# The per-layer projection placed ahead of the gate product

## The reference, cut to what matters

```python
h = h + 0.5 * rmsnorm_2(swiglu(rmsnorm_2(h, norm_g[0]), ffn1_gu, ffn1_down), norm_g[1])
...                                     # the token mixer, norms 2 and 3
h = h + 0.5 * rmsnorm_2(swiglu(rmsnorm_2(h, norm_g[4]), ffn2_gu, ffn2_down), norm_g[5])
gate = jax.nn.sigmoid(rmsnorm_2(h, norm_g[6]) @ ple_gate)
h = h + rmsnorm_2((p_i @ ple_proj) * gate, norm_g[7])
```

## Time and profile before

| | |
|---|---|
| median of 3 runs | 2860.72 us (2858.97 to 2862.37) |
| the profiled execution | 2861.04 us |
| its span in the trace | 2858.9 us |
| mean granted TensorE clock | 0.966 of full |
| TensorE busy | 2662.3 us, 12320 products |
| POOL, DVE, ACT busy | 1037.0, 1144.5, 979.3 us |

### The profile page before, as it was taken

How to read it: one execution, slowest core, us unless ns; L and a number is a source line. 1 busy time by engine, 2 the same in 40 slices (tenths; PEclk the granted TensorE clock), 3 DMA queues, 4 the chain that set the end, 5 groups by cost and what they waited for, 6 DMA issues and landing times.

```text
span 2858.9 us, 32128 instructions
## 1 busy us (share of the span) xinstructions
PE 2662.3 (93%) x12320; PEld 2111.7 (74%) x12320; DVE 1144.5 (40%) x1735; ACT 979.3 (34%) x1419; POOL 1037.0 (36%) x444
## 2 busy tenths in 40 slices
PE   8899988888999999879999998999998969999996
PEld 2788766676888877657888876788877747888875
DVE  0788665524222036555222035322027574322025
ACT  2323323423323233444233234323233444323233
POOL 0223255433444432213444433444432203444432
PEclk9999999999999999979999999999999979999998
DMA  6212110032332322102333322333322102332321
GB/s 262 60 59 90 51 37 30 24 106 74 103 103 89 96 81 72 52 23 75 102 96 96 93 91 68 103 96 96 96 89 65 60 8 81 96 99 93 102 90 66
DMA packets 63331, 234.00 MB, mean 82 GB/s; under 512 B 7264, under 2 KB 7520, under 8 KB 62688
## 3 DMA queue, kind: packets, MB, share of 16 engines
q1 hardware_dynamic: 61056, 222.33, 24.6%
q10 hardware_dynamic: 2144, 9.80, 1.0%
HBM read 230.00 MB, written 2.10 MB: 81 GB/s over the span
## 4 chain that ended last, share of the span: by engine, by line
issue 58%; POOL 20%; PE 16%; DVE 3%; ACT 1%; DMA 1%; POOLq 1%; SPq 0%; DVEq 0%; ACTq 0%
POOL wlo L448 20%; PE banks L1904 2%; PE banks L1910 2%; PE banks L1905 2%; PE banks L1842 1%; PE banks L2024 1%; DMA ada_raw<-in_stream 1%; PE banks L1680 1%; PE banks L2031 1%; PE banks L1973 1%; PE banks L1975 1%; PE banks L1974 1%; PE banks L1908 1%; PE banks L1909 1%; PE banks L1994 1%
## 5 line engine op out<-in xcount | busy, mean ns | idle before, releaser
L448 POOL TENSOR_TENSOR wlo<-raw,whi 128x1024 fp32r<-128x1024 f32 x351 | 848.4, 2421 | 1418.7 <-ACT whi L478 1418.6
L1650 PE MATMUL banks<-xhi,whi 128*128 128x512 f32 x2016 | 800.4, 397 | 60.5 <-ACT xhi L502 30.1
L1651 PE MATMUL banks<-xhi,wlo 128*128 128x512 f32 x2016 | 793.1, 393 | 0.0
L1660 PE MATMUL banks<-xlo,whi 128*128 128x512 f32 x2016 | 762.3, 394 | 5.7 <-DVE xlo L983 5.7
L478 ACT ACTIVATE whi<-raw 128x1024 fp32r<-128x1024 f32 x396 | 415.6, 1054 | 375.6 <-PE banks L1660 367.6
L1650 PEld LDWEIGHTS banks<-xhi,whi 128*128 128x128 f32 x2016 | 383.3, 190 | 157.5 <-issue 57.0
L1660 PEld LDWEIGHTS banks<-xlo,whi 128*128 128x128 f32 x2016 | 380.2, 189 | 94.2 <-DVE xlo L983 11.9
L1651 PEld LDWEIGHTS banks<-xhi,wlo 128*128 128x128 f32 x2016 | 383.7, 190 | 80.0 <-issue 1.3
L1650 PE MATMUL banks<-act_hi,whi 128*128 128x512 f32 x704 | 273.9, 389 | 0.0
L1651 PE MATMUL banks<-act_hi,wlo 128*128 128x512 f32 x704 | 273.9, 389 | 0.0
L1660 PE MATMUL banks<-act_lo,whi 128*128 128x512 f32 x704 | 273.9, 389 | 0.0
(11 more groups left out here) (368 smaller groups left out, 3140.1 us busy)
## 6 DMA issues: line engine op xcount, KB each, us to landing
raw<-in_stream SPq DMA_DIRECT2D x396, 512.0 KB, 3.5
ada_raw<-in_stream SPq DMA_DIRECT2D x24, 512.0 KB, 9.1
h<-in_x ACTq DMA_DIRECT2D x2, 2048.0 KB, 12.2
out<-h SPq DMA_DIRECT2D x4, 512.0 KB, 2.6
ctx_raw<-in_ctx ACTq DMA_DIRECT2D x1, 1024.0 KB, 19.5
dft_t<-in_dft_t ACTq DMA_DIRECT2D x1, 1024.0 KB, 4.8
ple_raw<-in_ple ACTq DMA_DIRECT2D x2, 512.0 KB, 3.5
mixpar<-in_mixpar ACTq DMA_DIRECT2D x2, 384.0 KB, 4.1
```

What stands on the lines that cost most here:

```text
L448: pool.tensor_tensor(wlo[:, i], raw[:, i], whi[:, i].bitcast(F32), ALU.subtract)\
L1650: pe.matmul(acc[acc_of[t]][:], whi[:, u % SLOTS, i], x_h, start=(k == 0), stop=False)
L1651: pe.matmul(acc[acc_of[t]][:], wlo[:, u % SLOTS, i], x_h, start=False, stop=False)
L1660: mm = pe.matmul(acc[acc_of[t]][:], whi[:, u % SLOTS, i], x_l, start=False, stop=(k == k_tiles - 1))
```

## The change

The projection goes ahead of the gate product, behind the down product of s = 2. TensorE runs two of its tiles, then the sum of squares of the down output, then the other six tiles. DVE copies each projection tile out of PSUM into a new buffer `projected_ple` before it begins `boundary`. `ple` is loaded at the start of s = 2 into other memory, and `ple_hi` and `ple_lo` are made during the gate-up tiles of s = 2 (pairs 4 and 6). In s = 3 DVE scales each gate tile straight into `y_dyn`, ACT takes the sigmoid in place, DVE multiplies by `projected_ple` one tile behind, and ACT squares one tile behind; the table for Ln and Exp is loaded again behind the last sigmoid. In `norm_in` the gate's units are cast behind the projection's.

```diff
     STREAM += [(("gu", _layer, 0), 2 * FT, KT), (("down", _layer, 0), KT, FT),
                (("in2", _layer), IN_T, KT), (("out2", _layer), KT, KT),
                (("gu", _layer, 1), 2 * FT, KT), (("down", _layer, 1), KT, FT),
-               (("gate", _layer), KT, KT), (("proj", _layer), KT, PLE_T)]
+               (("proj", _layer), KT, PLE_T), (("gate", _layer), KT, KT)]
 WHOLE_UNITS = ADA_T * KT // UNIT
...
         mod_rows = at("mod_rows", DYN + 25 * KB, [D * 3])
         c_silu = at("c_silu", DYN + 24 * KB, [KT, 2])
-        ple_raw = at("ple_raw", DYN + 16 * KB, [PLE_T, SEQ])
-        ple_hi = at("ple_hi", DYN + 20 * KB, [PLE_T, SEQ], F32R)
-        ple_lo = at("ple_lo", DYN + 24 * KB, [PLE_T, SEQ], F32R)
+        ple_raw = at("ple_raw", 36 * KB, [PLE_T, SEQ])
+        ple_hi = at("ple_hi", 40 * KB, [PLE_T, SEQ], F32R)
+        ple_lo = at("ple_lo", 44 * KB, [PLE_T, SEQ], F32R)
+        projected_ple = at("projected_ple", DYN + 16 * KB, [KT, SEQ])
         ident = table[:, C_ID:C_ID + P]
         ones = table[:, C_ONE:C_ONE + P]
...
             def norm_in(q, gain):
+                if q[1] == 3:
+                    high_parts(units_to(q))
                 high_parts(units_to(q) + SLOTS)
                 for k in range(KT):
                     if k == 5:
...
             for layer in range(DEPTH):
                 for s in range(4):
                     q = (layer, s)
-                    if s == 3:
+                    if s == 2:
                         act.dma_start(ple_raw[:, :, :], a["ple"][layer].rearrange("p (k t) -> p k t", t=SEQ))\
                             .then_inc(ld[f"ple{layer}"], 16)
...
                             act.activation(tmp[0][:], tmp[0][:], ACT.Silu).then_inc(*done("silu", (q, j)))
                             act.wait_ge(*after("act_formed", (q, j)))
                             act.activation(act_hi[:, j], tmp[1][:], ACT.Copy).then_inc(*done("act_high", (q, j)))
+                            if s == 2 and j == 4:
+                                act.wait_ge(ld[f"ple{layer}"], 16)
+                                act.activation(ple_hi[:, :, :], ple_raw[:, :, :], ACT.Copy)\
+                                    .then_inc(*done("ple_high", layer))
                         y_out(("down", layer, s // 2), q, FT, y_over_x)
                     elif s == 1:
...
                     else:
                         for m in range(KT):
                             tile_ready(("gate", layer), m, KT)
-                            if m == 3:
-                                act.wait_ge(ld[f"ple{layer}"], 16)
-                                act.activation(ple_hi[:, :, :], ple_raw[:, :, :], ACT.Copy)\
-                                    .then_inc(*done("ple_high", layer))
                             act.wait_ge(*after("gate2_scaled", (layer, m)))
-                            act.activation(y_dyn[:, m], tmp[m % 2][:], ACT.Sigmoid)\
+                            act.activation(y_dyn[:, m], y_dyn[:, m], ACT.Sigmoid)\
                                 .then_inc(*done("gate2", (layer, m)))
+                            if m:
+                                act.wait_ge(*after("y_formed", (q, m - 1)))
+                                squares("y_sq", q, m - 1, y_dyn[:, m - 1])
                         log_and_exp()
-                        for m in range(KT):
-                            tile_ready(("proj", layer), m, PLE_T)
-                            act.wait_ge(*after("y_formed", (q, m)))
-                            squares("y_sq", q, m, y_dyn[:, m])
+                        act.wait_ge(*after("y_formed", (q, KT - 1)))
+                        squares("y_sq", q, KT - 1, y_dyn[:, KT - 1])
                         inverse_root((("post", q), D, norm_bank[:], inv_rms[:]))
             high_parts(units)
...
                         boundary("first", None, q, par1[:, P1_FIN:P1_FIN + KT], gains(layer, 2 * s))
                     else:
                         y = y_over_x if before[1] in (0, 2) else y_dyn
+                        if s == 3:
+                            for m in range(KT):
+                                t = first_tile["proj", layer] + m
+                                v.wait_ge(*after("product", (("proj", layer), m)))
+                                v.tensor_copy(projected_ple[:, m], acc[acc_of[t]][:]).then_inc(*done("ple_out", (layer, m), bank_of=t))
                         boundary(before, y, q, gains(before[0], 2 * before[1] + 1), gains(layer, 2 * s))
                     if s == 1:
                         hgrn_clear(layer)
...
                             v.wait_ge(*after("act_high", (q, j)))
                             v.tensor_tensor(act_lo[:, j], tmp[1][:], act_hi[:, j].bitcast(F32), ALU.subtract)\
                                 .then_inc(*done("act_low", (q, j)))
+                            if s == 2 and j == 6:
+                                v.wait_ge(*after("ple_high", layer))
+                                v.tensor_tensor(ple_lo[:, :, :], ple_raw[:, :, :], ple_hi[:, :, :].bitcast(F32),
+                                                ALU.subtract).then_inc(*done("ple_low", layer))
                         for m in range(KT):
                             sq_add("y_sq", q, m)
                     elif s == 1:
...
                         for m in range(KT):
                             sq_add("y_sq", q, m)
                     else:
+                        def gated(m):
+                            v.wait_ge(*after("gate2", (layer, m)))
+                            v.tensor_tensor(y_dyn[:, m], y_dyn[:, m], projected_ple[:, m], ALU.mult)\
+                                .then_inc(*done("y_formed", (q, m)))
+                            if m:
+                                sq_add("y_sq", q, m - 1)
+
                         for m in range(KT):
                             t = first_tile["gate", layer] + m
                             v.wait_ge(*after("product", (("gate", layer), m)))
-                            if m >= 2:
-                                v.wait_ge(*after("gate2", (layer, m - 2)))
-                            v.tensor_tensor(tmp[m % 2][:], acc[acc_of[t]][:], inv_rms[:], ALU.mult)\
+                            v.tensor_tensor(y_dyn[:, m], acc[acc_of[t]][:], inv_rms[:], ALU.mult)\
                                 .then_inc(*done("gate2_scaled", (layer, m), bank_of=t))
-                            if m == 4:
-                                v.wait_ge(*after("ple_high", layer))
-                                v.tensor_tensor(ple_lo[:, :, :], ple_raw[:, :, :], ple_hi[:, :, :].bitcast(F32),
-                                                ALU.subtract).then_inc(*done("ple_low", layer))
-                        for m in range(KT):
-                            t = first_tile["proj", layer] + m
-                            v.wait_ge(*after("product", (("proj", layer), m)))
-                            v.wait_ge(*after("gate2", (layer, m)))
-                            v.tensor_tensor(y_dyn[:, m], y_dyn[:, m], acc[acc_of[t]][:], ALU.mult)\
-                                .then_inc(*done("y_formed", (q, m), bank_of=t))
                             if m:
-                                sq_add("y_sq", q, m - 1)
+                                gated(m - 1)
+                        gated(KT - 1)
                         sq_add("y_sq", q, KT - 1)
                     before = q
             boundary(before, y_dyn, "last", gains(DEPTH - 1, 7), None)
...
                         product(("out2", layer), KT, KT, xhi, xlo, "mix", lambda k: (layer, k))
                     else:
                         product(("gate", layer), KT, KT, xhi, xlo, "x", tile, pre_sum, True)
-                        product(("proj", layer), KT, PLE_T, ple_hi, ple_lo, "ple", lambda k: layer)
-                    sum_squares(("post", q), "y_sq", q)
+                    if s == 2:
+                        post_sum = lambda m: sum_squares(("post", q), "y_sq", q) if m == 1 else None
+                        product(("proj", layer), KT, PLE_T, ple_hi, ple_lo, "ple", lambda k: layer, after_tile=post_sum)
+                    else:
+                        sum_squares(("post", q), "y_sq", q)
     return ev.values, ev.freed
...
             if s == 0:
                 weights.append(leads_first(blocks_of(i["w_in_2"][l][:, order])))
                 weights.append(blocks_of(i["w_out_2"][l][order_out]))
+        weights.append(blocks_of(i["ple_proj_2"][l]))
         weights.append(leads_first(blocks_of(i["ple_gate_2"][l])))
-        weights.append(blocks_of(i["ple_proj_2"][l]))
     par = np.zeros((DEPTH, P, P2_COLS), np.float32)
     mix = np.zeros((DEPTH, P, M2_COLS), np.float32)
     for l in range(DEPTH):
```

## The result

The kernel after takes **2866.9 us** (median of 20 executions, 2865.2 to 2874.8), the one before 2861.3 us in the same sessions (20 executions, 2856.8 to 2864.7). The medians differ by 5.6 us, where 5.4 were forecast. The ratio is 1.0025 with a 95% interval of 1.0019 to 1.0032, about 7 us. It lies above the quotient of the medians because five of the 20 executions after took 2873 to 2875 us, which a median doesn't see; the means differ by 7.4 us. The execution that was profiled after the change took 2870.4 us (span 2868.6), 3.5 more than its median; the one before took 2861.04. The traces have therefore 9.4 us to account for, not 5.6.

The account below looks back on a forecast made before the run. TensorE, busy 93% of the span, was taken to bound the kernel. Per layer -0.9 - 0.05 + 1.2 + 1.7 + 0.8 = +2.7, two layers +5.4 on the 2860.72 us median: 2866.1 us, range 2857 to 2870.

Parts of the forecast that it names:

- The move: Projection put behind the down product: 10.89 us go at layer end, first residual step +9.9 later; -0.9 us a layer.
- The held first addition: Seam: DVE's addition of k=0 waits for a whole POOL subtraction; TensorE restarts 4.6 us behind the first residual step.
- First step to tile 4: First residual step to gate tile 4: 30.7 us, -0.1 us for both layers together, bounds -2.9 to +2.
- The casts moved into s = 2: `ple_hi` and `ple_lo` at gate-up pairs 4 and 6 cost nothing; without idle cover, 2.6 us a layer.
- The sixth cast: Gate stage: squares delay ACT's cast of the sixth unit, so `wlo` and tile 5 come +1.2 us late a layer.
- the clock behind tile 5: After a 2.5 us wait at gate tile 5, 3.4 us at half clock lose +1.7 us a layer.
- The tail: Last gate product to Ln: 7.0 us where last projection product to Ln was 6.14; +0.8 us a layer.
- The copies did not wait for POOL: Rival on the moved projection: PSUM copies do wait for POOL, +1.6 us a layer, 2869.3 us; chance 0.10.
- Square and sigmoid need no load between them: Rival on the gate: square and sigmoid need different tables, each alternation loads 1.3 us, 2878.5 us; chance 0.05.
- No fall at tile 5: Rival: clock does not fall behind gate tile 5's wait, all else as forecast, +2.0, 2862.7 us; chance 0.18.
- The sum: All terms: +2.7 us a layer, +5.4 for two; 2866.4 us for the profiled execution, 2866.1 for the median; chance 0.50.
- the gate's terms: Gate stage a layer: +1.2 us for the late sixth unit and +1.7 us for half clock behind tile 5.

Follow-up runs that it names:

- Experiment 2: Kernel after, with ACT's cast of the gate's third unit moved behind the input casts of k=0 and k=1: 2866.3 us, ratio 1.0012 to the kernel before.
- experiment 3: Kernel after, with ACT casting the gate's sixth unit right behind the first sigmoid: 2862.0 us, ratio 1.0001 to the kernel before.
- experiment 4: Kernel after, without the one-tile lag from gate tile 4 on and Ln's table loaded behind the last square: 2865.1 us, ratio 1.0005 to the kernel before.
- experiment 1: Kernel after, with DVE's copies spread through the residual steps and the third unit's cast moved later: 2866.4 us, ratio 1.0012 to the kernel before.
- 7: Kernel after, with the eight projection copies on ACT instead of DVE, third unit's cast behind k=1: 2859.6 us, ratio 0.9990 to the kernel before.
- 6: Kernel after, with the edits of experiments 2, 3 and 4 together: 2857.3 us, ratio 0.9990 to the kernel before.
- 8: Kernel after, with the edits of experiments 7, 3 and 4 together: 2853.2 us, ratio 0.9968 to the kernel before.
- experiment 5: Kernel before, with ACT casting the gate's sixth unit behind the first sigmoid, not at tile 3: 2857.0 us, ratio 0.9984 to the kernel before.

## Why the forecast was right, point by point

- **The move, -0.9 us a layer.** Shown: the first residual step 13.68 us behind the last down product (forecast 13.6), the projection without a gap but for the sum. A copy takes 0.69 us and the next instruction starts 0.61 behind it, as taken.
- **The held first addition.** Shown: 2.71 us against "2.5 or more", TensorE back 4.39 us behind the first step (forecast 4.6). Experiment 2 took the hold away and the wait shrank by the same 2.02 us, but TensorE reached tile 4 only 0.3 to 0.4 us sooner at an equal clock.
- **First step to tile 4, 30.7 us: mis-sized.** This is the term of the sum that failed: 31.9 and 32.2 us, so +2.6 for both layers where -0.1 stood, beyond the +2 that bounded it. The forecast let the restart be followed by 3.4 us of low clock, partly inside the wait, and charged 0.7 us; it was 6.8 us in both layers (from 1697.98 and 2790.25), of which 5.2 and 6.0 lay behind the restart: 2.6 and 3.0 us. Smaller errors went the other way: a restart 0.2 us sooner, and 1.29 us instead of 1.9 for the wait at tile 4. Its own rows gave the warning: a PEclk of 0.87 over 27 us in layer 0 is 3.5 us lost, or 7 us at half clock, twice what it took from layer 1. With 3.4 us of low clock the stretch takes what was forecast: 30.8 in both layers of experiment 3 and 30.9 in layer 1 of experiment 4, whose seam is that of the kernel after, with the same wait of 5.03 us. Layer 0 of experiment 4 had 6.8 us of it and took 32.25. Why the clock stayed low for a second 3.4 us in one layer and not in the other is open.
- **The casts moved into s = 2, nothing.** Shown: from the Ln of its input norm to the last down product s = 2 takes 340.8 or 340.9 us in both layers of both kernels.
- **The sixth cast, +1.2 us, and the clock behind tile 5, +1.7 us.** Shown, slightly smaller: the cast 5.20 us behind the first scaling (5.3), the wait 2.32 us (2.5), 3.4 us at half clock in both layers, +2.6 and +2.7 together. Experiment 3 parts them into 1.6 and 1.6, and layers that had the wait without the low clock took 24.2 or 24.3 us from t4 to the last gate product, halfway between 22.7 and 25.9. That the wait decides isn't the whole truth: of the ten layers in which tile 5 waited 2.32 to 2.35 us (the kernel after and experiments 1, 2, 4 and 7), six had the low clock behind it and four had not (layer 1 of experiments 2 and 4, both layers of 7). That both layers of the profiled execution had it was partly luck.
- **The tail, +0.8 us.** Shown: 7.02 and 7.20 us to Ln (7.0), the sum starting when the last addition is in. Experiment 4 took away the lag of one tile and moved the table load, and Ln came at 5.22. The lag was the cause: in the kernel after, the square behind the table load ended at 1757.25, while the first half of the sum held TensorE until 1758.4.
- **The rivals.** The copies did not wait for POOL (0.69 us at 1689.14, under POOL's 4.76). Square and sigmoid need no load between them: each gate stage alternates between them with one load at its start (L942, 1727.11) and one ahead of Ln (L511, 1755.33). The Trainium skill (ScalarE: Activation LUTs, section "Table sets: the hidden batching unit") has cheap functions in every set; its list doesn't name square, and the trace shows square to be no exception. "No fall at tile 5" was wrong in the profiled execution, but it happens, as experiments 2, 4 and 7 show.
- **The sum.** The profiled execution came to 2870.4 us where 2866.4 were forecast: 2.7 us are the mis-sized term and 1.5 the longer low clock in layer 1's mixer, where nothing was changed; against them the gate's terms were 0.5 too large in all, and the tail's 0.1 too small. The median came to 2866.9, 0.8 from the forecast. So the median execution loses some 3.5 us less than the one in the trace, and where is not visible, as only one was profiled. The mechanisms are shown; that the total agrees within 1 us is partly luck, since the means differ by 7.4 us and the low clock, in places that the change doesn't touch, moved single executions by more than 1 us.

## What to carry to other kernels

Moving work into a gap fills it only if the chain that ends the gap doesn't start again behind the moved work: here eight copies, in order, stood ahead of the residual steps on the very engine that bounds the seam, and the gap came back longer (5.03 us, 3.85 before). Look at what the moved step does to the queues of the engines that were idle; the copies on ACT, one cast put ahead of two squares, and a tail without lag turned 0.25% slower into 0.32% faster. When a wait grows from about 1.3 to 2.3 us, count the clock as well as the wait, as something that may or may not come, and don't add up repairs whose gains rest on it. And cut two traces into the same stretches before explaining a total: 1.5 of the 9.4 us here came from a stage that nobody had changed.

## What the runs showed that was not expected

- Low-clock stretches came in lengths of about 3.4 us (1735.5 to 1739), 6.8 us (1698 to 1705), 10.2 us (behind layer 0's tail in experiments 3, 4, 6 and 8) and 13.7 us (1755 to 1769 in experiment 1). The same wait was followed by different lengths: 2.36 us by 3.4 us of half clock in the kernel before and by none in experiment 5; 5.03 us by 6.8 in the kernel after, by 3.4 in experiment 3, and by 6.8 in layer 0 and 3.4 in layer 1 of one execution in experiment 4.
- The time of one kernel spreads with the clock: experiment 3's executions lie between 2856.2 us, at a mean granted clock of 0.967, and 2867.8, at 0.960. Experiment 5's lie between 2855.1 and 2857.6; why they spread less is not shown.
- A hold of DVE by POOL doesn't go away when the subtraction is issued later. It passes to the next DVE instruction that has two inputs in SBUF (2.71 us on the addition of `h`, 2.89 on the one into `sq_sum`); copies out of PSUM beside it took their 0.69 us.
